# The first 128 tokens take no part in the matmuls with U: rows of U are made on chip, fetched, and multiplied on VectorE

## The chip, the cores and the metric

One core of a Trainium2 chip runs the whole program in one launch. The metric is the time of that launch on the device in microseconds; smaller is better. The program is the same on every run, and the time before is the median of three runs.

## The reference

Two layers of a decoder trunk with 512 tokens of width 1024, in float32. Each layer has a mixer (three parallel token mixers behind one wide projection, merged by gates), cross attention on 256 memory tokens, and PEER, a retrieval over 16384 experts of one neuron each:

```python
def peer(h, wq, keys, u_tab, v_tab):
    q = (h @ wq).reshape(bsz, length, 8, 2, 128)
    s = jnp.einsum('blhpd,hpkd->blhpk', q, keys)
    s_top, i_top = lax.top_k(s, 16)
    cand = s_top[..., 0, :, None] + s_top[..., 1, None, :]      # 16 x 16
    best, pos = lax.top_k(cand.reshape(..., 256), 16)           # per head
    gates = jax.nn.softmax(best, axis=-1)
    act = jax.nn.gelu(jnp.einsum('bthkd,btd->bthk', u_tab[idx], h)) * gates
    return jnp.einsum('bthk,bthkd->btd', act, v_tab[idx])
```

Every token so uses 8 x 16 = 128 experts, and for each a row of `u_tab` and a row of `v_tab`, both 1024 wide.

## The kernel before

All matmuls of any size are split into three products of a high and a low part (`fp32r`), so a weight tile passes ScalarE (the high part, a cast) and VectorE (the low part, a subtraction) before TensorE takes it. Each stage is a `Block` in which every engine runs its own list of instructions in order, tied to the others by semaphores. SyncE issues all plain DMAs in order, GpSimd the indirect ones.

**The projections** (`Linear`, lines 208 to 355; used by `normed_stage`, `linear_stage`, `gates_stage`, `residual_stage`, `keys_stage`). A weight tile of 2 MB has four units. For each unit ScalarE makes `w_hi` (L301), VectorE `w_lo` (L306), TensorE does 24 matmuls of 512 columns (L280 or L289). High and low parts have two buffers, so `w_lo` of a unit is made during the matmuls of the unit before, when those before that are done. SyncE loads a weight tile each four units and otherwise waits. In the mixer the first three stages are such projections, of 28, 8 and 24 units; `gates_stage` also stores each finished 1 MB tile of gates.

**Other stages**: HGRN, retention, S5 (`ssm_stage`, in which VectorE copies four row groups, then turns eight groups of injections, and SyncE copies 64 KB pieces with 32 DMAs, L1103), merge (24 short units of 12 matmuls), the output projection with the residual, then the query, attention (`attend_stage`, four heads) and its output.

**The keys stage** makes the scores and the top 16 keys for each head and side.

**The experts stage** (`experts_stage`) holds two loops of 128 tiles; a tile is 128 experts.

*The U loop.* Per tile n: SyncE loads U (512 KB, feature-major, three buffers), ScalarE makes `uh` (L1914), VectorE `ul` (L1986), TensorE does 24 matmuls of 512 columns, all tokens (L1856), ScalarE takes the GELU (L1920), SyncE stores the 128 x 512 result to `gelu_of_dots` in HBM. Beside this VectorE chooses the experts: `choose_keys` (tiles 2 to 5), then for each of four blocks of 128 tokens, eight tiles a block from tile 7: `pick_heads` (top 16 of 256 candidates for two heads, by MAX8, FIND_INDEX8 and MATCH_REPLACE8), `mark`, `soften`, `add_up` (a reduction, L2022). GpSimd makes the candidate sums (L1822) and the numbering product (L1831). From tile 45 to 92 VectorE makes the hot rows (`make_hot`, `weigh`: two 128x2048 f16 operations a tile, L2074, L2077, L2082), TensorE multiplies them to a dense table of gates (24 times 32 matmuls, L1877), and SyncE stores it in 12 pieces of 2 MB, one in four tiles, the last at tile 97. At tile 122 (`V0`) SyncE waits for gates and dots to be stored and loads the first three V tiles.

*The V loop.* Tokens 128 to 511 go through TensorE: activations times gates, split into parts, 18 matmuls of 512 columns a tile (L1888), with all rows of V. Tokens 0 to 127 stand apart (`APART = P`): each has a list of 128 experts; GpSimd fetches for list place c one dot per token from `gelu_of_dots` (L1843) and one row of V per token (L1844) into one of three buffers, and VectorE adds dot x gate x row to `acc` (`join`: L2052, L2058). In layer 0 VectorE also makes the tables of layer 1's S5 here.

SyncE's list in the U loop:

```python
for n in range(PK):
    if 1 <= n and n + 2 < PK:
        load_u(n + 2)
    if n:
        store_dots(n - 1)
    c, r = divmod(n - HOT0 - 8, 4)
    if 0 <= c < NH and r == 0:
        store_gates(c)
    if n == V0:
        ...
```

Of the kernel before, what the change touches and what calls it, by code (L numbers as in the profile page):

```python
# [35 lines left out]
SLOTS = PH * TOPK  # L36
GCH = 64
# [3 lines left out]
RING = 3  # L41
LEVELS = [64, 32, 16, 8, 4, 2, 1]
# [164 lines left out]

class Linear:
# [34 lines left out]
    def sync(self, sp, following=None, behind=None):  # L243

        def load(t, p, first):
            if not first:
                sp.wait_ge(self.s["lo_done"], (t - 1) * 4)
                self.weights.load(sp, t, p)
            if behind is not None and t >= 2:
                behind(sp, t - 2)  # L250
        over_pairs(sp, self.n, load)
        if following is not None:
            for t in (self.n, self.n + 1):
                sp.wait_ge(self.s["lo_done"], (t - 1) * 4)
                following.load(sp, t % 2, t % 2)
        if behind is not None:
            for t in range(max(self.n - 2, 0), self.n):
                behind(sp, t)
# [85 lines left out]
    def vector(self, v, copy=None, beside=None):  # L344
# [32 lines left out]
def setup_stage(nc, io, m, mem):  # L377

    with ExitStack() as ctx, stage(nc, "loaded", "dve_step", "angles_ready", "trig_ready") as s:
# [10 lines left out]
        with nc.Block() as block:  # L390
            @block.sync
            def _(sp):
                for dst, src in loads:
                    sp.dma_start(dst, src).then_inc(s["loaded"], 16)

# [123 lines left out]
def normed_stage(nc, m, gain, weights, act, psum, copy, following=None, ahead=None):  # L519


    with ExitStack() as ctx, stage(nc, *LINEAR_SEMS, *Norm.SEMS, "first_unit", weights=weights) as s:
        norm = Norm(nc, ctx, m, s, m.X, TB, [gain], [act], psum)
        lin = Linear(nc, ctx, s, "fm", weights, act, TB, T, psum, norm)
        with nc.Block() as block:
            @block.sync
            def _(sp):
# [3 lines left out]
                lin.sync(sp, following)  # L531
# [14 lines left out]
            def _(v):  # L546
# [3 lines left out]
                lin.vector(v)  # L550


def linear_stage(nc, kind, weights, act, nb, N, psum, copy, on="scalar", following=None):
    with ExitStack() as ctx, stage(nc, *LINEAR_SEMS, weights=weights) as s:
        lin = Linear(nc, ctx, s, kind, weights, act, nb, N, psum)
        with nc.Block() as block:
            block.sync(lambda sp: lin.sync(sp, following))
            block.tensor(lin.tensor)
            block.scalar(lambda a: lin.scalar(a, copy if on == "scalar" else None))
            block.vector(lambda v: lin.vector(v, copy if on == "vector" else None))  # L560
# [507 lines left out]
def ssm_stage(nc, m, sm, tabs, u, work, spare, rows, w_glu, psum):  # L1068
# [5 lines left out]
    with ExitStack() as ctx, stage(nc, "dve_step", "rows_mm", "sorted_even", "sorted_odd", "turn_mm", "turn_copied", "w_mm", "w_copied",  # L1074
                                   "inj_mm", "inj_turned", "scanned", "block_mm", "block_copied", "toep_in0", "toep_in1",
                                   "swap_mm", "states_in", "y_mm", "y_taken", "y_done", "yt_mm", "yt_copied",
                                   "out_mm", "out_copied", "glu_in") as s:
# [9 lines left out]
        wmat = [sb(f"wmat{i}", [P, 2, 2, P]) for i in range(2)]  # L1087
        om_, yb, st_ = (x.rearrange("p a t -> p (a t)").rearrange("p (g n) -> p g n", n=N5) for x in work)
# [8 lines left out]
        with nc.Block() as block:  # L1097
            @block.sync
            def _(sp):
                for c in range(NB):  # L1100
# [6 lines left out]
                sp.wait_ge(s["glu_in"], 16)  # L1107

# [118 lines left out]
            def _(v):  # L1227
                st = Steps(v, s["dve_step"])
                for b in range(NB):
                    v.wait_ge(s["rows_mm"], 2 * b + 2)  # L1230
                    sort_rows(v.tensor_copy, 2 * b + 1).then_inc(s["sorted_odd"], 1)
                for c in range(G5 // 4):
# [4 lines left out]
                    v.tensor_tensor(f2(om_)[:, cs], f2(om_)[:, cs], f2(st_)[:, cs], ALU.add).then_inc(s["inj_turned"], 1)  # L1237
                v.wait_ge(s["inj_turned"], G5 // 4)
# [1290 lines left out]
```

## Time and profile before

| | us |
|---|---|
| median of 3 runs | 4937.71 (4930.27 to 4955.9) |
| the profiled execution's own time | 4943.19 |
| its span in the profile | 4941.3 |
| TensorE busy | 4498.7 (91%) |
| TensorE weight loads | 3655.4 (74%) |
| VectorE busy | 2812.0 (57%) |
| ScalarE busy | 1698.1 (34%) |
| GpSimd busy | 816.6 (17%) |
| moved by DMA | 842.86 MB, 171 GB/s |

The page also cuts the span in 40 equal slices and gives each as a digit: tenths busy, tenths of TensorE's full clock, and GB/s. The two V loops are the slices of 263 to 350 GB/s; elsewhere the core moves 29 to 209 GB/s.

```profile
## 2 busy tenths in 40 slices
PE   5699888879999999988989997897999999999998
PEclk9899988999999999999999998898999999999999
DMA  4322114202445664887973221312224466479997
GB/s 179 145 101 111 47 71 128 102 29 83 143 144 177 209 197 160 320 295 283 350 297 119 85 107 71 94 69 85 90 91 145 154 204 207 164 263 346 338 350 270
```

A busy share of TensorE is that of instructions whose ends are modelled, so what a matmul costs in a stream is read from the distance between starts, not from its length.

### The profile page before, as it was taken

Reading aid. Unit: us, or ns where it says so; the run is one execution under the profiler, and the core shown is the slowest. Engines: PE = TensorE matmul, PEld = TensorE weight load, DVE = VectorE, ACT = ScalarE, POOL = GpSimd, SP = SyncE. Lnnn points to the kernel's source line nnn. Section 1 sums busy time; section 2 is a strip of 40 time slices with the busy share of each in tenths; the row PEclk is TensorE's granted clock in tenths of the full one; section 3 lists DMA queues with packets and bytes.
Section 4 is the critical chain, followed back from the end, with each engine's and each line's share of the span. In section 5 each row is a group of like instructions: output and inputs, shape, how many; then the busy total and the mean of one; then the engine's idle time right before and its main releaser. Section 6 shows DMA issues by size and latency. Waiting matters only on the chain. (4 is left out here: it accounts for less than half of the span.)

```text
span 4941.3 us, 54367 instructions
## 1 busy us (share of the span) xinstructions
PE 4498.7 (91%) x21288; PEld 3655.4 (74%) x21288; DVE 2812.0 (57%) x4695; ACT 1698.1 (34%) x2131; POOL 816.6 (17%) x588
## 2 busy tenths in 40 slices
PE   5699888879999999988989997897999999999998
PEld 4577766657888888766767775675778888887776
DVE  6522544427885532799872226353589554258887
ACT  3323222223335542332323232323233455233333
POOL 0000210000210000454530003000011000025554
PEclk9899988999999999999999998898999999999999
DMA  4322114202445664887973221312224466479997
GB/s 179 145 101 111 47 71 128 102 29 83 143 144 177 209 197 160 320 295 283 350 297 119 85 107 71 94 69 85 90 91 145 154 204 207 164 263 346 338 350 270
DMA packets 349246, 842.86 MB, mean 171 GB/s; under 512 B 31296, under 2 KB 191808, under 8 KB 333632
## 3 DMA queue, kind: packets, MB, share of 16 engines
q1 hardware_dynamic: 303936, 705.00, 40.7%
q0 software_dynamic: 45056, 134.38, 7.3%
q8 instruction: 170, 2.79, 0.2%
q14 instruction: 84, 0.69, 0.0%
HBM read 683.56 MB, written 151.52 MB: 169 GB/s over the span
## 5 line engine op out<-in xcount | busy, mean ns | idle before, releaser
L1986 DVE TENSOR_TENSOR ul<-u,uh 128x1024 fp32r<-128x1024 f32 x256 | 365.4, 1428 | 630.5 <-ACT uh L1914 628.3
L306 DVE TENSOR_TENSOR w_lo<-w,w_hi 128x1024 fp32r<-128x1024 f32 x200 | 244.3, 1225 | 729.3 <-ACT w_hi L301 728.0
L1888 PE MATMUL psum<-vh,ah 128*128 128x512 f32 x1536 | 486.3, 398 | 83.2 <-DVE al L2094 83.0
L1856 PE MATMUL psum<-h_lo,uh 128*128 128x512 f32 x2048 | 516.2, 394 | 13.3 <-DVE ul L1986 13.3
L1843 POOL DMA_INDIRECT pick_d<-gelu_of_dots,pick x256 | 276.2, 1079 | 1492.2 <-DMA gelu_of_dots<-ge 1076.2
L1856 PE MATMUL psum<-h_hi,ul 128*128 128x512 f32 x2048 | 506.3, 389 | 0.0
L1856 PE MATMUL psum<-h_hi,uh 128*128 128x512 f32 x2048 | 505.7, 389 | 0.0
L1888 PE MATMUL psum<-vl,ah 128*128 128x512 f32 x1536 | 479.8, 394 | 0.0
L1888 PE MATMUL psum<-vh,al 128*128 128x512 f32 x1536 | 478.2, 393 | 0.0
L1856 PEld LDWEIGHTS psum<-h_lo,uh 128*128 128x128 f32 x2048 | 381.6, 189 | 92.9 <-DVE ul L1986 15.8
L1945 ACT CAST vh<-v 128x1024 fp32r<-128x1024 f32 x256 | 269.3, 1052 | 524.2 <-PE psum L1888 444.7
L1856 PEld LDWEIGHTS psum<-h_hi,ul 128*128 128x128 f32 x2048 | 384.5, 188 | 81.0
L1856 PEld LDWEIGHTS psum<-h_hi,uh 128*128 128x128 f32 x2048 | 384.4, 188 | 79.8
L1888 PEld LDWEIGHTS psum<-vh,ah 128*128 128x128 f32 x1536 | 286.2, 191 | 167.7 <-DVE vl L2092 107.0
L1920 ACT ACTIVATE ge<-psum 128x512 f32<-128x512 f32 x256 | 153.7, 600 | 699.5 <-PE psum L1856 698.8
L2092 DVE TENSOR_TENSOR vl<-v,vh 128x1024 fp32r<-128x1024 f32 x256 | 312.9, 1222 | 123.8 <-ACT vh L1945 123.4
L1844 POOL DMA_INDIRECT rows<-in_peer_v,pick x256 | 333.6, 1303 | 88.0 <-issue 88.0
L1888 PEld LDWEIGHTS psum<-vl,ah 128*128 128x128 f32 x1536 | 292.3, 190 | 62.8
L1888 PEld LDWEIGHTS psum<-vh,al 128*128 128x128 f32 x1536 | 291.9, 190 | 62.5
L2058 DVE SCALAR_TENSOR_TENSOR acc<-rows,pick_d,acc 128x1024 f32<-128x1024 f32 x254 | 326.3, 1285 | 9.5 <-DVE pick_d L2052 0.5
L1914 ACT CAST uh<-u 128x1024 fp32r<-128x1024 f32 x256 | 266.6, 1043 | 171.1 <-DMA u<-in_peer_u 169.5
L301 ACT CAST w_hi<-w 128x1024 fp32r<-128x1024 f32 x200 | 209.2, 1050 | 183.6 <-PE psum L289 169.9
(421 smaller groups left out, 6817.7 us busy)
## 6 DMA issues: line engine op xcount, KB each, us to landing
u<-in_peer_u SPq DMA_DIRECT2D x256, 512.0 KB, 3.7
v<-in_peer_v SPq DMA_DIRECT2D x256, 512.0 KB, 6.2
gelu_of_dots<-ge SPq DMA_DIRECT2D x256, 256.0 KB, 2.2
gates_by_group<-held SPq DMA_DIRECT2D x24, 2048.0 KB, 9.8
act<-gelu_of_dots SPq DMA_DIRECT2D x64, 768.0 KB, 7.5
gate<-gates_by_group SPq DMA_DIRECT2D x64, 768.0 KB, 9.7
w<-in_w_fm SPq DMA_DIRECT2D x12, 2048.0 KB, 8.1
w<-in_w_gate SPq DMA_DIRECT2D x12, 2048.0 KB, 8.1
```

Of the source, the lines that this page charges most:

```text
L301: a.copy(self.shaped(self.hi[q % 2]), self.unit_of(p, q)).then_inc(self.s["hi_done"], 1)
L306: v.tensor_tensor(self.shaped(self.lo[q % 2]), self.unit_of(p, q), self.shaped(self.hi[q % 2]).bitcast(F32), ALU.subtract).then_inc(self.s ...
L1843: pool.indirect_dma_start(pick_d[:, c:c + 1], None, every_dot, bass.IndirectOffsetOnAxis(ap=pick[:, 1, c:c + 1], axis=0)).then_inc(m.rows_ ...
L1844: pool.indirect_dma_start(rows[c % NG][:], None, every_v, bass.IndirectOffsetOnAxis(ap=pick[:, 0, c:c + 1], axis=0)).then_inc(m.rows_picke ...
L1856: mm = nc.tensor.matmul(dot_bank(n), w[r][:, k, :], h[:, k, :], start=(x == 0 and k == 0), stop=(x == 2 and k == KD - 1))
L1888: mm = nc.tensor.matmul(sum_bank(b, half), q[p][:, b * P:(b + 1) * P], w[p][:, half * W:(half + 1) * W], start=(n == 0 and x == 0), stop=( ...
L1914: a.copy(fw(uh[r]), u[r][:]).then_inc(s["u_hi"], 1)
L1920: a.activation(ge[n % 2][:], dot_bank(n), ACT.Gelu_apprx_tanh).then_inc(s["gelu_done"], 1)
L1945: a.copy(vh[p][:], vv[n % VR][:]).then_inc(s["v_hi"], 1)
L1986: v.tensor_tensor(fw(ul[r]), u[r][:], fw(uh[r]).bitcast(F32), ALU.subtract).then_inc(s["u_lo"], 1)
L2058: v.scalar_tensor_tensor(acc[:], rows[c % NG][:], pick_d[:, c:c + 1], acc[:], ALU.mult, ALU.add).then_inc(s["joined"], 1)
L2092: v.tensor_tensor(vl[p][:], vv[n % VR][:], vh[p][:].bitcast(F32), ALU.subtract).then_inc(s["v_lo"], 1)
```

## The change

Tokens 0 to 127 leave the U loop's matmuls as they had left the V loop's.

1. *Turned rows of U.* U lies in HBM feature-major, for the matmuls. The new class `Turns` loads a tile of 512 KB, turns its 32 x 32 blocks with one VectorE transpose, and stores it with four DMAs (32 partitions each, runs of 256 numbers) as rows in `m.u_rows[l]`. It has two raw and one or two (in some stages three or four) outgoing buffers. The features of a row so lie in another order, and `h0`, the normed tokens in that order, is made to match in the keys stage. 124 of the 128 tiles of each layer are turned beside the projections, S5, merge and attention of that layer, 4 in its keys stage. Each stage ends with a wait for its stores.
2. *The dots of tokens 0 to 127.* For list place c GpSimd fetches one row of U per token in the U loop (one of four buffers), VectorE multiplies it with `h0` and sums it up (`dot`), 128 times over the tiles 21 to 127; ScalarE takes the GELU in four chunks. The dense result and `gelu_of_dots` now have 384 columns. The fetch of single dots goes. The rows of V follow in the same ring right behind.
3. *The choosing.* 80 of the 256 candidates remain (those that can be in the top 16), GpSimd does none of it, the reduction becomes four additions, and the steps are laid out anew: keys at tiles 1, 3, 5, 8, the first block from 10, the others from 20 to 74 in steps of 9/4 tiles, hot rows from 75 in steps of 11/12 tile, the last table store at 122, `V0` at 123.
4. `gates_stage` holds its gates in halves; the list of SyncE in `Linear.sync` goes by units; the gains of the expert norm go to HBM as a row in the setup.

The core of the diff:

```diff
+class Turns:
+    def load(self, sp, x):
+        if x < self.n:
+            if x >= 2:
+                sp.wait_ge(self.s["row_turned"], x - 1)
+            sp.dma_start(self.raw[x % 2], self.src(x)).then_inc(self.s[f"turn_in{x % 2}"], 16)
...
+    def behind(self, sp, u):
+        for x in [x for x in range(self.n) if self.after[x] == u]:
+            p = x % len(self.out)
+            sp.wait_ge(self.s["row_turned"], x + 1)
+            for b in range(P // S):
+                sp.dma_start(self.dst(x)[b], self.out[p][b * S:(b + 1) * S].rearrange("p (f w) -> p f w", f=P // S)).then_inc(self.s[f"turn_out{p}"], 16)
+            self.load(sp, x + 2)
+
+    def turn(self, v, u):
+        for x in [x for x in range(self.n) if self.after[x] == u]:
+            p = x % len(self.out)
+            v.wait_ge(self.s[f"turn_in{x % 2}"], 16 * (x // 2 + 1))
+            if x >= len(self.out):
+                v.wait_ge(self.s[f"turn_out{p}"], 16 * (P // S) * (x // len(self.out)))
+            v.transpose(self.out[p],
+                        self.raw[x % 2].rearrange("p (k f w) -> p f k w", k=KD, w=S)).then_inc(self.s["row_turned"], 1)
+
+    def done(self, sp):
+        for p in range(len(self.out)):
+            sp.wait_ge(self.s[f"turn_out{p}"], 16 * (P // S) * len(range(p, self.n, len(self.out))))
...
+        for u in range(4 * self.n):
+            t = u // 4 + 2
+            if u % 4 == 3 and (t < self.n or following is not None):
+                sp.wait_ge(self.s["lo_done"], u + 1)
...
+            if turns is not None:
+                turns.behind(sp, u)
...
+                if turns is not None:
+                    turns.turn(v, t * 4 + q)
...
+                turns.start(sp)
+                for x in range(3 * NB):
+                    turns.behind(sp, x)
                 for c in range(NB):
                     sp.wait_ge(s["block_copied"], 2 * c + 2)
...
+                    if n == 2:
+                        v.wait_ge(s["gain_in"], 16)
+                        as_rows = lambda x: x.rearrange("p (k b w) -> p b k w", k=KD, b=P // S)
+                        v.tensor_tensor(h0[:].rearrange("p (b k w) -> p b k w", b=P // S, k=KD), as_rows(norm.xn[:, 0, :]), as_rows(gain_row[:]), ALU.mult)
...
+KEYS_AT = [1, 3, 5, 8]
+HOT0, V0, JOIN0 = 75, 123, 4
...
-                    pool.indirect_dma_start(pick_d[:, c:c + 1], None, every_dot, bass.IndirectOffsetOnAxis(ap=pick[:, 1, c:c + 1], axis=0)).then_inc(m.rows_picked[c % NG], 16)
-                    pool.indirect_dma_start(rows[c % NG][:], None, every_v, bass.IndirectOffsetOnAxis(ap=pick[:, 0, c:c + 1], axis=0)).then_inc(m.rows_picked[c % NG], 16)
+                for x in range(2 * SLOTS):
+                    if x >= NG:
+                        before = x - NG
+                        if before < SLOTS:
+                            pool.wait_ge(s["dotted"], before + 1)
+                        else:
+                            pool.wait_ge(s["joined"], before - SLOTS + 1)
+                    c = x % SLOTS
+                    pool.indirect_dma_start(rows[x % NG], None, m.u_rows[l] if x < SLOTS else every_v,
+                                            bass.IndirectOffsetOnAxis(ap=pick[:, x // SLOTS, c:c + 1], axis=0)).then_inc(m.rows_picked[x % NG], 16)
...
-                            mm = nc.tensor.matmul(dot_bank(n), w[r][:, k, :], h[:, k, :], start=(x == 0 and k == 0), stop=(x == 2 and k == KD - 1))
+                            mm = nc.tensor.matmul(dot_bank(n), w[r][:, k, :], h[:, k, T0:], start=(x == 0 and k == 0), stop=(x == 2 and k == KD - 1))
...
+                def dot(c):
+                    v.wait_ge(m.rows_picked[c % NG], fetched(c))
+                    v.scalar_tensor_tensor(rows[c % NG], rows[c % NG], 1.0, h0[:], ALU.mult, ALU.mult,
+                                           accum_out=pick_d[:, c:c + 1]).then_inc(s["dotted"], 1)
...
-                normed_stage(nc, m, sm[:, 0:KD], w_fm, h, psum, fm_out, following=w_tm)
+                normed_stage(nc, m, sm[:, 0:KD], w_fm, h, psum, fm_out, turning(sorted([*range(2, 28), *range(5, 28, 4)])),
+                             tm[:].rearrange("p (a b) n -> p a (b n)", b=2), following=w_tm)
```

## Rows read from the trace of the kernel before

**Rows 1.** The page, part 1: busy time of each engine.

```profile
PE 4498.7 (91%) x21288; PEld 3655.4 (74%) x21288; DVE 2812.0 (57%) x4695; ACT 1698.1 (34%) x2131; POOL 816.6 (17%) x588
```

**Rows 2.** Busy time by stretch: stretch, length, engines with counts, clock, DMA share, GB/s.

```profile
215.00:345.00 130.00, 130.00 (x561) 105.42 (x560) 28.60 (x24) 41.05 (x54) 0.00 (x0) 1.00 0.26 97
1342.00:1500.00 158.00, 157.07 (x697) 129.54 (x696) 132.44 (x206) 52.92 (x71) 32.08 (x7) 1.00 0.43 145
1600.00:1700.00 100.00, 100.00 (x630) 83.65 (x629) 53.07 (x47) 54.32 (x38) 0.00 (x0) 1.00 0.67 209
1976.00:2350.00 374.00, 330.81 (x1373) 261.10 (x1373) 327.96 (x494) 118.17 (x158) 189.55 (x156) 0.97 0.82 299
2350.00:2530.00 180.00, 166.05 (x712) 133.97 (x711) 143.42 (x205) 63.21 (x82) 97.53 (x85) 0.98 0.96 360
4500.00:4920.00 420.00, 403.42 (x1754) 328.66 (x1753) 348.90 (x498) 145.09 (x194) 237.50 (x199) 1.00 0.91 334
```

**Rows 3.** Matmuls of U and V by line: durations, first and last start.

```profile
L1856 PE MATMUL psum<-h_lo,uh x2048: 387/389/794, 1229.4 to 4370.0; 128*128 128x512 f32 x187
L1888 PE MATMUL psum<-vh,ah x768: 387/389/767, 1977.0 to 2588.9; 128*128 128x512 f32 x192
L1888 PE MATMUL psum<-vh,ah x768: 389/389/628, 4373.8 to 4923.0; 128*128 128x512 f32 x192
```

**Rows 4.** TensorE in order of time, 256 and 512 columns, products; a weight load.

```profile
61.83 1.12 PE L2307 MATMUL psum<-memT_hi,w_lo 128*128 128x256 f32 x8
62.79 1.12 PE L2307 MATMUL psum<-memT_hi,w_hi 128*128 128x256 f32 x8
...
L2307 PEld LDWEIGHTS psum<-memT_hi,w_lo x128: 188/192/330, 49.2 to 140.1; 128*128 128x128 f32 x128
...
1403.47 1.98 PE L1856 MATMUL psum<-h_hi,ul 128*128 128x512 f32 x8
1405.29 1.98 PE L1856 MATMUL psum<-h_hi,uh 128*128 128x512 f32 x8
...
1756.98 2.02 PE L1877 MATMUL psum<-part,hot_j 128*128 128x128 f16 x32
```

**Rows 5.** Groups of VectorE by shape: busy us, mean ns, idle before.

```profile
L2058 DVE SCALAR_TENSOR_TENSOR acc<-rows,pick_d,acc 128x1024 f32<-128x1024 f32 x254 | 326.3, 1285 | 9.5 <-DVE pick_d L2052 0.5
L2082 DVE TENSOR_TENSOR part<-hot_i,lists 128x2048 f16<-128x2048 f16 x96 | 113.0, 1219 | 0.0
L2022 DVE TENSOR_REDUCE out<-hot 128x128 f32<-128x2048 f16 x16 | 65.1, 4069 | 0.0
L2052 DVE TENSOR_TENSOR pick_d<-pick_d,pick_w 128x1 f32<-128x1 f32 x256 | 40.0, 156 | 66.6 <-DMA rows<-in_peer_v,pick 64.8
L1564 DVE MAX8 val<-sc 128x8 f32<-128x128 f32 x128 | 27.8, 279 | 0.2
L1564 DVE MAX8 best<-cand 128x8 f32<-128x256 f32 x64 | 23.9, 415 | 0.0
```

**Rows 6.** DMA issues with us to landing, and GpSimd's wait before its gathers.

```profile
u<-in_peer_u SPq DMA_DIRECT2D x256, 512.0 KB, 3.7
gates_by_group<-held SPq DMA_DIRECT2D x24, 2048.0 KB, 9.8
...
POOL pick_d L1843 <- DMA gelu_of_dots<-ge: 1076.2, 2, 538.6
```

**Rows 7.** VectorE in order of time in the first projection.

```profile
283.24 1.23 DVE L306 TENSOR_TENSOR w_lo<-w,w_hi 128x1024 fp32r<-128x1024 f32 x1 [4.35 <-ACT w_hi L301]
288.82 1.23 DVE L306 TENSOR_TENSOR w_lo<-w,w_hi 128x1024 fp32r<-128x1024 f32 x1 [4.36 <-ACT w_hi L301]
```

**Rows 8.** S5: a stretch of its copies, SyncE's issues, VectorE at an injection.

```profile
750.00:755.00 5.00, 5.00 (x24) 2.23 (x23) 4.93 (x4) 2.00 (x2) 0.00 (x0) 1.00 0.75 94
...
743.44 21.76 SPq L1103 DMA_DIRECT2D toep<-fm  x32
...
721.27 0.42 DVE L1235 TENSOR_TENSOR fm<-psum,tcos 128x256 f32<-128x256 f32 x1 [1.81 <-PE psum L1145]
```

More of the change, by code:

```diff
@@ L241, in first_loads, with sync @@
         self.weights.load(sp, 1, 1)
[L243 to L258, printed above, removed]
+    def sync(self, sp, following=None, behind=None, turns=None):
+        for u in range(4 * self.n):
+            t = u // 4 + 2
+            if u % 4 == 3 and (t < self.n or following is not None):
+                sp.wait_ge(self.s["lo_done"], u + 1)
+                if t < self.n:
+                    self.weights.load(sp, t, t % 2)
+                else:
+                    following.load(sp, t % 2, t % 2)
+            if behind is not None:
+                behind(sp, u)
+            if turns is not None:
+                turns.behind(sp, u)
     def tensor(self, pe):
@@ L1099, in _ @@
             def _(sp):
+                turns.start(sp)
+                for x in range(3 * NB):
+                    turns.behind(sp, x)
                 for c in range(NB):
@@ L1231, in _ @@
                     sort_rows(v.tensor_copy, 2 * b + 1).then_inc(s["sorted_odd"], 1)
+                    turns.turn(v, b)
                 for c in range(G5 // 4):
@@ L1320, in _ @@
             def _(sp):
-                lin.sync(sp, None, rest_tile)
-                for p in range(2):
-                    sp.wait_ge(rested[p], 16 * (weights.n // 2))
+                turns.start(sp)
+                lin.sync(sp, None, rest_behind, turns)
+                rest_half(sp, weights.n - 1, 1)
+                for half in range(2):
+                    sp.wait_ge(rested[half], 16 * weights.n)
+                turns.done(sp)
             block.tensor(lin.tensor)
@@ L1383, in _ @@
             def _(sp):
-                for t in range(2, weights.n + 2):
-                    sp.wait_ge(s["w_lo"], HALF * (t - 1))
-                    if t < weights.n:
-                        weights.load(sp, t, t % 2)
-                    else:
-                        following.load(sp, t - weights.n, t % 2)
+                turns.start(sp)
+                for n in range(NU):
+                    if n % HALF == HALF - 1:
+                        t = n // HALF + 2
+                        sp.wait_ge(s["w_lo"], n + 1)
+                        if t < weights.n:
+                            weights.load(sp, t, t % 2)
+                        else:
+                            following.load(sp, t - weights.n, t % 2)
+                    turns.behind(sp, n)
+                turns.done(sp)
             @block.tensor
@@ L1461, in _ @@
                         sum_low(n - 19)
+                    turns.turn(v, n)
                 weigh(NU - 1)
@@ L1475, in attend_stage, with _ @@
         pt = [sb(f"probT{i}", [P, MB, T]) for i in range(2)]
+        turns = turning(s, ctx, None)
         mx, sm_, rc = sb("mx", [P, XH, TB]), sb("sme", [P, XH, TB]), sb("rc", [P, XH, TB])
         with nc.Block() as block:
+            @block.sync
+            def _(sp):
+                turns.start(sp)
+                for x in range(3 * XH):
+                    turns.behind(sp, x)
+                turns.done(sp)
             @block.tensor
@@ L1717, in experts_stage @@
                 ab = tmp("ab", [P, 2, SLOTS], F16)
-                hot = [two(f"hot{i}", hkk, F16) for i in range(2)]
+                rc = tmp("rc", [P, 2, SLOTS], F16)
+                far, wrap, near = (tmp(n, [P, SLOTS], F16) for n in ("far", "wrap", "near"))
+                hot = two("hot", hkk, F16)
                 numbers = tmp("numbers", [P, TOPK])
```

405 lines of the change are left out of this document (241 added, 164 removed).

## The prediction

> **What bounds the kernel now.** I read the page first, then the busy time by stage, then the time order inside one unit of each loop, then the DMA rows. TensorE is busy 91% of the span [rows 1], and by stage it is the limit almost everywhere that this change touches: 130 of 130 us in the first projection, 157 of 158 and 100 of 100 us in two stretches of the loop over U [rows 2]. The expert layer is two loops of 128 tiles. The U loop of layer 0 runs from 1229.4 to 1977.0 us (the first V matmul), 747.6 us, and that of layer 1 is alike. The V loops take 613 us in layer 0 and 551 in layer 1 [rows 3]. A U tile is 24 matmuls of 512 columns; eight of them follow each other in 1.81 us [rows 4], so a tile is 5.44 us and 128 tiles 696. The 24 products of the gate table (32 matmuls in 2.0 us each [rows 4]) bring it to 744. So the U loop is TensorE's, with no room. A V tile is 18 matmuls, 4.08 us, or 522 us a loop: layer 1 loses 29 us to waits, layer 0 loses 91, where VectorE also makes the tables of the next layer (328 of 374 us busy [rows 2]). All sums are against the profiled execution: span 4941.3, its own time 4943.2, which is 5.5 us over the median of the three.
>
> **U loop, TensorE.** 128 of the 512 columns go. The price of a column comes from the memory stage: eight matmuls of 256 columns take 0.96 us, 0.120 each, eight of 512 take 0.2265 each [rows 4]. That is 0.000416 us a column, so 384 columns take 0.173 us and a tile 4.16 us: 1.28 us less, 163.5 us a layer, **327 us** in both. A weight load of this size is shown as 0.192 us, longer than 0.173; but it is shown so beside the 256-column matmuls too, and they run 0.120 us apart [rows 4]. So the load is hidden and I take 0.173. The Trainium skill (TensorE: Matmul & The Clock Gate, Back-to-back issue gap) says that a stream of load and matmul pairs is spaced by both operations, which speaks against this change; the 0.120 us of this trace is against it for these sizes.
>
> **U loop, VectorE.** It loses GpSimd's company but gains its work. Per tile: `low_u` 1.2 us. Per token row, 128 of them over 106 tiles: one multiply with a row sum, 128x1024 with two inputs, priced as the accumulate at 1.285; that is 1.55 us a tile. The top-16 searches go from 256 to 80 candidates: an instruction takes 0.415 at 256 and 0.279 at 128 [rows 5], 0.051 off for another 48 gives 0.23. With overlap a pair of heads goes from 3.8 to about 2.0 us. The numbering comes over from GpSimd at 1.22 (two a block), and the 4.07 us reductions become four adds, about 1.5. A block of tokens costs about 20 us instead of some 31. Between tiles 21 and 74: 54 x (1.2 + 1.55) + 3 x 20 = 208 us against TensorE's 225. Between 75 and 119, where the hot rows are made (48 steps of 2.4): 115 + 45 x 2.75 = 239 us against TensorE's 45 x 4.16 + 48 = 235. So VectorE goes from half busy to level with TensorE, and I charge 8 us a layer for uneven tiles.
>
> **U loop, DMA.** Now 0.43 busy before the hot rows, 2.3 us for 0.79 MB a tile; 0.67 in them [rows 2], 4.3 us a tile of 6.4, so a 2 MB store of gates, one in four tiles, takes 8 us. The V rows and tiles run at 334 GB/s with 0.91 busy, 367 GB/s full, 1.43 us for 0.52 MB. After: U tile 1.43, dots 0.65 (384 of 512 columns of what is left of 2.3), 1.2 gathered rows 1.72, together 3.8 us in a tile of 4.16; in the hot tiles one store each 3.7 tiles adds 2.2, together **6.0 us against VectorE's 5.3**. DMA becomes the bound there: 45 x 0.7, +30 us a layer. At the tail the last gate store now leaves at tile 122 and SyncE waits for it at 123 (before: 97 and 122), with three V tiles and two groups ahead of the last two U tiles. Gates take 9.8 us to land [rows 6], 3 MB follow in 8 us: U tile 126 is about 22 us after 123 and wanted after 10, so +11. The first tiles: +1. **Given back: 50 us a layer**, bounds 15 (the engines share better than the sum) and 100. Net for the U loops: -227, bounds -297 and -127.
>
> **V loop.** The 256 gathers of one number and the small multiplies go (0.156 us and a gap, 24 us of VectorE a loop [rows 5]), the rows' first fetches are already under way. TensorE's 522 stays. Layer 0 is VectorE's: -20. Layer 1: -10 of its 29. **-30**, bounds -55 and -5.
>
> **The turns.** 124 of 128 tiles of a layer are turned outside the keys stage: 32 in the first projection, 8 and 28 in the next two, 12 each in S5, merge and attention, 20 in the two residuals and the query. Each adds a 0.5 MB load, a VectorE transpose, four stores and, on SyncE, five issues. No transpose is in the trace: the nearest rows are 1.285 for 1024 elements and two inputs and 4.07 for 2048 strided ones [rows 5], so 1.28 to 2.03 us; I take 1.3, since this one reads nearly in order too. The Trainium skill (VectorE: DVE Perf Modes, The three transpose paths) gives 0.31 us for a 128x128 block of 16-bit numbers; no run here shows it. In a projection unit of 5.58 us VectorE idles 4.35 us before each `w_lo` [rows 7], so one turn or two hide if their data is there. If it isn't, `w_lo` queues behind the wait on VectorE, and TensorE behind that. Whether it is there is DMA's question. Load 1.43; the stores have runs of 1 KB from 32 partitions. Dots, 2 KB runs from 128 partitions, would give 1.8 us for 0.5 MB; the copies from 16 partitions in S5 run at 94 GB/s with 0.75 busy [rows 8], 4.2 us. I take 2.2, nearer the dots since their destination is HBM too, so 3.6 us a turn. The three projections last about 325 us and need 68 x 3.6 + 15 weight tiles x 5.6 + 20 for gates = 349 us. That is **+24**, and +6 for uneven ones; bounds 5 and 165. S5: its first four turns meet a phase of 1.7 us a step and each pair waits for five issues (0.68 each by the S5 copies [rows 8]) and a landing (3.7 [rows 6]): +12; at the next eight VectorE idles 1.81 us each [rows 8], enough for the transpose. Merge +6, its VectorE being fuller; attention +3, other stages, with their stores awaited at the end, +4. **+55 a layer, +110**, plus 3 for the gains at the start. Bounds +30 and +410.
>
> **Sum:** -227 - 30 + 110 + 3 = -144 on 4941.3; median 4937.7 - 144 = **4795**, rounded to 5.
>
> **Rivals.**
> (a) *All of it hides.* Requests overlap better than my sums: U loops -290, V -45, turns +45: 4650. For it: DMA stands 0.96 busy at 360 GB/s in one stretch of the V loop while TensorE is 166 of 180 busy [rows 2]. Against it: 3.6 us x 68 has no room.
> (b) *The U loop passes to VectorE and DMA,* so that fewer columns buy little: VectorE level with TensorE and DMA 0.9 or more together cost another 45 us a layer: 4880. For it: the V loop of layer 0, where VectorE at 328 of 374 us leaves TensorE 331 [rows 2]. Against it: layer 1 loses only 5% with DMA 0.91 busy.
> (c) *Slower: the stores of the turned rows.* If their price is that of the S5 copies, a turn is 5.6 us, the projections need 68 x 5.6 + 104 = 485 us for 325: +160 a layer, S5, merge and attention +45: 4941 - 257 + 410 = 5090. It decides from the point where the turns give back 257 us, 128 a layer: 25 of these are fixed, so 103 / 68 = 1.5 us over the 3.25 us that are free (325 - 104 over 68), a turn of 4.8 us and a store of 3.3.
> (d) *The weight load sets the pace.* 24 x 0.192 = 4.61 us a tile, 57 us a layer less saved, of which 30 lie under the DMA's excess: 4850. Only the spacing of 0.120 us speaks against it, and it is clear.
>
> **Numbers.** Forecast 0.47 (4720 to 4850), (a) 0.18, (b) 0.20, (c) 0.10, (d) 0.05. About 0.5% (25 us) is what a measurement of this kernel can tell from no change. Of (b) a quarter lies within that: faster 0.85, same 0.05, slower 0.10. The range of 8 in 10 runs from 4640, under (a), to 4920, over (b).
>
> **What would show it.** Matmuls of line 1856's successor 0.17 us apart and U tiles 4.2 us apart before the hot rows, about 6.0 within them, with DMA at 0.9 or more; a gap of some 10 us in TensorE near tile 126; U loops of about 635 us. GpSimd's wait of 538 us before the gathers [rows 6] gone. The first three stages 25 to 30 us longer, with VectorE waiting for the raw tile of a turn at the double turns; transposes at 1.2 to 2.0 us. It is wrong if these stages grow by over 100 us a layer (then (c)), if the U tiles stay above 4.5 us before the hot rows with VectorE full (then (b)), or if the projections keep their length (then (a)).

## The result and the profile after

The change made the kernel 0.8% slower: 4975.4 us (4956.3 to 4982.7) against 4934.1 (4914.7 to 4955.9), a ratio of 1.008 with the interval 1.007 to 1.0094, where 4795 was forecast and 4640 to 4920 allowed for. The profiled execution spans 4977.0 us.

The page, part 1 and two lines of part 2, of the kernel after:

```profile
PE 4250.9 (85%) x21282; PEld 3630.8 (73%) x21282; DVE 3255.4 (65%) x5347; ACT 1662.7 (33%) x2135; POOL 758.1 (15%) x564
...
PEclk9899988989999988999999998799899998899999
DMA  4597726666288877988988882566536887789997
```

TensorE was relieved of 248 us [rows 1] and the span is 36 us longer all the same: the engine has less work and stands still for longer. Where, I read from the distance between the first matmuls of each stage, in both traces and in four kernels of the experiments, which are told below (us, the sum of the two layers; S5 runs to the start of merge, a V loop to the next projection or the end; HGRN, retention, the attention's own output and the keys are not in the table and moved by 6 us at most):

| stage | before | after | early | early_pool | moved_sync | noturn |
|---|---|---|---|---|---|---|
| three projections | 708.5 | 764.1 | 759.4 | 762.7 | 761.3 | 709.9 |
| S5 | 219.7 | 259.1 | 260.3 | 261.1 | 238.5 | 210.4 |
| merge | 156.5 | 187.0 | 185.4 | 185.0 | 187.3 | 157.3 |
| output and query | 217.6 | 220.9 | 222.4 | 221.6 | 236.8 | 218.0 |
| attention | 108.1 | 135.1 | 132.7 | 132.6 | 114.5 | 107.0 |
| U loops | 1495.8 | 1414.9 | 1278.2 | 1199.4 | 1198.1 | 1422.1 |
| V loops | 1195.0 | 1149.8 | 1145.2 | 1149.2 | 1144.4 | 1151.9 |
| span | 4941.3 | 4977.0 | 4827.1 | 4756.6 | 4731.6 | 4822.1 |

From before to after: U loops -81 (forecast -227), V loops -45 (-30), everything else +162 (forecast: turns +110 and setup +3). Two stretches of the U loop of layer 0 after the change, ahead of the hot rows and in them (columns as in [rows 2]):

```profile
1410.00:1640.00 230.00, 225.12 (x1294) 223.09 (x1293) 200.54 (x449) 90.39 (x124) 94.75 (x64) 1.00 0.90 314
1640.00:1980.00 340.00, 259.14 (x1871) 252.23 (x1870) 226.41 (x253) 151.91 (x118) 83.48 (x56) 0.88 0.78 254
```

Ahead of the hot rows all is as forecast. In them TensorE stands for 81 of 340 us, its clock is 0.88, and no engine is full: VectorE 226, DMA 0.78. Something makes all of them wait. The waits of that stretch (us in total, how many, the longest), then ScalarE, SyncE and TensorE in order of time around one of them:

```profile
POOL rows L1963 <- DVE rows L2199: 252.4, 47, 16.5
ACT uh L2032 <- DMA u<-in_peer_u: 174.0, 26, 15.7
DVE ul L2110 <- ACT uh L2032: 111.3, 20, 10.5
PE psum L1997 <- ACT held L2060: 76.5, 13, 11.8
```

```profile
1789.18 0.49 ACT L2038 ACTIVATE ge<-psum 128x384 f32<-128x384 f32 x1 [2.25 <-PE psum L1976]
1800.83 1.04 ACT L2032 CAST uh<-u 128x1024 fp32r<-128x1024 f32 x1 [11.15 <-DMA u<-in_peer_u]
1801.78 3.72 ACT L2060 ACTIVATE held<-psum 128x2048 f32<-128x2048 f32 x1
```

```profile
1777.73 0.66 SPq L1905 DMA_DIRECT2D gelu_of_dots<-ge  x1
1778.43 0.43 SPq L1901 DMA_DIRECT2D u<-in_peer_u  x1
1786.03 0.32 SPq L1905 DMA_DIRECT2D gelu_of_dots<-ge  x1
1786.39 0.62 SPq L1909 DMA_DIRECT2D gates_by_group<-held  x1
1787.05 6.26 SPq L1901 DMA_DIRECT2D u<-in_peer_u  x1
1793.35 1.12 SPq L1905 DMA_DIRECT2D gelu_of_dots<-ge  x1
1794.52 0.94 SPq L1901 DMA_DIRECT2D u<-in_peer_u  x1
1805.84 0.32 SPq L1905 DMA_DIRECT2D gelu_of_dots<-ge  x1
```

```profile
1797.83 1.55 PE L1976 MATMUL psum<-h_hi,uh 128*128 128x384 f32 x8
1805.64 3.57 PE L1997 MATMUL psum<-part,hot_j 128*128 128x128 f16 x32 [6.26 <-ACT held L2060]
```

These rows show a loop of waits. SyncE's list for tile n is: load U tile n+2, store the dots of n-1, perhaps a store of gates. The load of tile n+2 so stands behind the store of dots n-2, which waits for its GELU, and ScalarE wants the tile one tile of work later, ahead of GELU n. If it isn't there, GELU n, the copy of the gate table and the store of dots n queue behind that wait, and with them the load of tile n+4. A landing (5.5 us in the median after, 6.7 in this stretch, 3.7 before [rows 6]) must fit in about one tile, which is now 4.2 us of TensorE's work, or 5.2 with its share of the products. And the issue that follows a store of gates is held up: 6.26 us here, 5.5 to 9.6 us at all 24 stores; and SyncE, done with its next load at 1795.5, waits 10 us for a GELU, which stands behind ScalarE's wait of 11.15 us for a U tile. TensorE then runs its 32 products at half the pace (3.57 us for 2.0).

The kernel before has the same held-up issues (5.4 to 7.0 us, all 24), and nothing shows that they cost it anything: TensorE works 100 of 100 us among them [rows 2]. The same place there, SyncE in order of time:

```profile
1706.83 0.43 SPq L1772 DMA_DIRECT2D gates_by_group<-held  x1
1707.31 5.79 SPq L1764 DMA_DIRECT2D u<-in_peer_u  x1
1713.86 0.51 SPq L1768 DMA_DIRECT2D gelu_of_dots<-ge  x1
```

How much each part of a U loop takes over TensorE's own work (4.16 us a tile, 2.0 a product) can be read from the starts of its tiles; layer 0, layer 1, in us:

| tiles of the U loop | forecast | after | early | pool | early_pool |
|---|---|---|---|---|---|
| 0 to 74, ahead of the hot rows | 1 | 10, 13 | 3, 3 | 7, 10 | 4, 3 |
| 75 to 121, the hot rows | 30 | 101, 96 | 37, 39 | 64, 59 | 0, 0 |
| 122 to 127, the tail | 11 | 16, 18 | 18, 18 | 25, 24 | 16, 16 |

(The forecast has 8 more for VectorE, at no place.) In the hot rows of the kernel after a tile takes 7.3 us on the mean, against 6.0 forecast.

### The profile page after: what moved, and what is told of

The parts are those of the page before. It is cut to its first block and busy times, and to the rows that moved or that the text cites. A ratio compares the mean times of both kernels' runs of the same rounds, so it can differ in the third digit from the quotient of the medians.

```text
span 4977.0 us, 56515 instructions
## 1 busy us (share of the span) xinstructions
PE 4250.9 (85%) x21282; PEld 3630.8 (73%) x21282; DVE 3255.4 (65%) x5347; ACT 1662.7 (33%) x2135; POOL 758.1 (15%) x564
## 5 line engine op out<-in xcount | busy, mean ns | idle before, releaser
L1963 POOL DMA_INDIRECT rows<-rows_of_u,pick x256 | 374.0, 1461 | 2223.8 <-DVEq L2195 1387.4
L2110 DVE TENSOR_TENSOR ul<-u,uh 128x1024 fp32r<-128x1024 f32 x256 | 313.0, 1224 | 377.3 <-ACT uh L2032 376.2
L1976 PE MATMUL psum<-h_lo,uh 128*128 128x384 f32 x2048 | 425.5, 351 | 51.9 <-DVE ul L2110 51.8
L1963 POOL DMA_INDIRECT rows<-in_peer_v,pick x256 | 287.6, 1124 | 792.3 <-DVE acc L2216 709.5
L1976 PE MATMUL psum<-h_hi,ul 128*128 128x384 f32 x2048 | 402.2, 338 | 0.0
L1976 PE MATMUL psum<-h_hi,uh 128*128 128x384 f32 x2048 | 396.7, 334 | 0.0
L1976 PEld LDWEIGHTS psum<-h_hi,ul 128*128 128x128 f32 x2048 | 365.8, 191 | 0.0
L1976 PEld LDWEIGHTS psum<-h_hi,uh 128*128 128x128 f32 x2048 | 359.1, 188 | 0.0
L253 DVE STREAM_TRANSPOSE turn<-turn 128x1024 f32<-128x1024 f32 x146 | 181.1, 1241 | 223.0 <-DMA turn<-in_peer_u 156.6
L2199 DVE SCALAR_TENSOR_TENSOR rows<-rows,h 128x1024 f32<-128x1024 f32 x256 | 308.8, 1218 | 2.0
## 6 DMA issues: line engine op xcount, KB each, us to landing
gates_by_group<-held SPq DMA_DIRECT2D x24, 2048.0 KB, 12.7
```

The source lines that it names most:

```text
L253: v.transpose(self.out[p], self.raw[x % 2].rearrange("p (k f w) -> p f k w", k=KD, w=S)).then_inc(self.s["row_turned"], 1)
L1963: pool.indirect_dma_start(rows[x % NG], None, m.u_rows[l] if x < SLOTS else every_v, bass.IndirectOffsetOnAxis(ap=pick[:, x // SLOTS, c:c ...
L1976: mm = nc.tensor.matmul(dot_bank(n), w[r][:, k, :], h[:, k, T0:], start=(x == 0 and k == 0), stop=(x == 2 and k == KD - 1))
L2110: v.tensor_tensor(fw(ul[r]), u[r][:], fw(uh[r]).bitcast(F32), ALU.subtract).then_inc(s["u_lo"], 1)
L2199: v.scalar_tensor_tensor(rows[c % NG], rows[c % NG], 1.0, h0[:], ALU.mult, ALU.mult, accum_out=pick_d[:, c:c + 1]).then_inc(s["dotted"], 1)
```

## Experiments

The kernel before was measured anew beside each group of experiments and its median went from 4934.1 to 4924.6 us, while the kernel after was measured beside the first of these values alone; so a difference from it is good to some 10 us.

**Theory A**: the order of SyncE's queue. **Rival B**: DMA throughput, as the prediction had it for the hot tiles. **Rival C**: VectorE, now level with TensorE. The first four kernels tell them apart and price the turns.

*early*: only the order of the loads changes.

```diff
-                    if 1 <= n and n + 2 < PK:
-                        load_u(n + 2)
+                    if n + 3 < PK:
+                        load_u(n + 3)
```

> SyncE issues the load of each U tile one tile sooner (tile n+3 instead of n+2, before the store of the dots of tile n-1); nothing else changes. Theory A (order of SyncE's queue): in the kernel after, the load of U tile n+2 stands behind the store of the dots of tile n-2, which waits for ScalarE's gelu, and ScalarE needs the tile one tile later, so landing (5.5 us) plus a blocked issue behind a store of gates (6 to 9 us) stalls the loop. Then the hot stretch 1640:1980, 340 us at 259 us of TensorE, shrinks by 50 to 80 us a layer: 4975 - 100 to 160, about 4840. Rival B (DMA throughput is the bound of the hot tiles): the same bytes, so the same time within 15 us: 4975. Rival C (VectorE is the bound of the hot tiles): the same, 4975.

4836.1 us, 0.981 of before (0.978 to 0.984) and 139 less than after, as theory A had it. The U loops give 137 of it. No byte and no VectorE work is gone, so B and C can't account for this part. The stretch of the hot rows:

```profile
1640.00:1940.00 300.00, 257.21 (x1888) 250.79 (x1888) 222.60 (x253) 158.03 (x121) 82.42 (x58) 0.94 0.92 306
```

*pool*: only the issuer of the 24 stores of gates changes.

```diff
-                    for c in stores_at[n]:
-                        store_gates(c)
...
+                def store_gates(c):
+                    pool.wait_ge(s["gate_copied"], 2 * c + 2)
+                    pool.dma_start(gates_dram[:, :, c, :].rearrange("g p x -> p g x"),
...
+                    while stored < NH and (x >= SLOTS + NG or x >= NG and min(stores_at_c[stored], PK) <= dot_at(x - NG)):
+                        store_gates(stored)
+                        stored += 1
```

> The 12 stores of gates a layer (2 MB each) are issued by GpSimd between its gathers instead of by SyncE; the U loads stay where they were. Theory A in its narrow form (the issue behind a store of gates blocks SyncE for 6 to 9 us): 24 stores x 6 us less, if each was felt in full: about -100 to -140, 4850. If only the missing lead of the loads counts and the block is secondary: -30 to -60. Rival B (DMA throughput) and rival C (VectorE): 4975 within 15 us.

4908.1 us, 0.995 (0.994 to 0.997), 67 less than after: half to two thirds of what the narrow form asked for, a little over the other. No issue of a U load takes over 2 us any more, and GpSimd's issue of a store of gates takes 1.75. The edit also takes SyncE's wait for the copied gates out of its list, but that wait was worth nothing: in the kernel after SyncE issues each of the 24 stores 0.04 us behind the issue ahead of it. The Trainium skill (DMA: Bandwidth & Descriptors, Issuing engines are not separate DMA queues) says that DMAs of all engines interleave on the same 16 DMA engines, and that another issuer saves only the sequencer's time, "which is usually small relative to the DMA itself". No run here tests the first half. Against the second, the time saved on SyncE was 5.5 to 9.6 us a store, beside 12.7 us from the issue of a store of gates to its landing, and worth 67 us.

*nofetch*: of the 128 fetches of rows of U in a layer only the first four are made, and VectorE multiplies these four again and again; the fetches of V then wait for the last multiply. The dots of tokens 0 to 127 are left wrong.

```diff
-                for x in range(2 * SLOTS):
+                for x in [*range(NG), *range(SLOTS, 2 * SLOTS)]:
...
-                    v.wait_ge(m.rows_picked[c % NG], fetched(c))
+                    v.wait_ge(m.rows_picked[c % NG], fetched(c % NG))
...
```

> Of the 128 gathers of U rows a layer only the first four are done; VectorE multiplies these four again and again (the dots of the first 128 tokens are left wrong), so its work and its order stay. 62 MB a layer less traffic during the U loop, a third of it. Rival B (DMA throughput is the bound of the hot tiles): -30 us to -60 a layer, about 4880. Theory A: a landing gets shorter, but the order stays: -10 to -30 a layer. Rival C (VectorE): no change, 4975.

4885.8 us, 90 less than after, 46 to 50 a U loop: inside B's range, not A's. So the traffic does matter. U tiles land after 3.9 us in the median here, against 5.5, so it can work by way of the landing, within A's loop of waits; this run alone doesn't tell the two apart. But a third of the traffic gone gives less than one reordered line.

*noturn*: no turns. In this run, and in *nostore* and *quarter*, the rows are fetched from U as it is given, and the dots of tokens 0 to 127 are left wrong.

```diff
-        self.s, self.after, self.first = s, after, m.rows_made[l]
+        self.s, self.after, self.first = s, [], m.rows_made[l]
...
-        self.n = len(after)
+        self.n = 0
...
```

> All 248 turns outside the keys stage and those inside it are left out (no load, transpose or store of them); the U rows are fetched from the U given in DRAM, which has them in another order, so the dots of the first 128 tokens are left wrong. It prices the turns by stage: I read about 158 us for both layers from the two traces (three projections 55, S5 40, merge 30, attention 25, others 8). If they are the turns' own: 4975 - 158 = 4817, and every stage as long as before the change. If part of the growth is a lower clock or DMA traffic that comes from elsewhere: 4860 or more. The U loop (708 us) should not change.

4821.2 us, 154 less. In the sum of both layers every stage of the table but S5 and the loops is within 1.5 us of its length before; S5 is 9 shorter, all of it in layer 0, where this profile shows a granted clock of 0.96 in the stage and before one of 0.86. The U loops gain nothing by it. The turns cost about what the stages showed.

The next four ask what is left in early, whether before had this loss too, and of what a turn's price is made.

*early_pool*: both edits.

> Both: U loads one tile sooner on SyncE, and the stores of gates issued by GpSimd. The run early brought a U loop from 708 to 638 us, the run pool to 676, each against about 595 us of TensorE work (128 tiles of 4.16 and 24 products of 2). Theory A (what is left in early, stalls of 5 to 8 us at some stores of gates, is the blocked issue behind these stores): 600 to 615 us a U loop, 4836 - 50 to 70 = about 4775. Rival B (what is left is DMA throughput, 0.94 busy in the hot stretch): no more than 10 us a loop below early, 4820 to 4836.

4760.5 us, 0.967 (0.964 to 0.969), 76 less than early. The U loops take 600.6 and 598.8 us, and the hot rows nothing over TensorE's own work: 5.2 us a tile. ScalarE's wait in the hot stretch, the stretch itself, and GpSimd in order of time:

```profile
ACT uh L2040 <- DMA u<-in_peer_u: 39.1, 23, 3.0
```

```profile
1640.00:1900.00 260.00, 250.63 (x1946) 246.15 (x1944) 226.18 (x257) 163.83 (x120) 112.55 (x71) 0.99 0.99 356
```

```profile
1702.98 1.68 POOL L1971 DMA_INDIRECT rows<-rows_of_u,pick  x1 [2.88 <-DVE rows L2207]
1704.65 1.75 POOL L1955 DMA_DIRECT2D gates_by_group<-held  x1
1707.53 1.71 POOL L1971 DMA_INDIRECT rows<-rows_of_u,pick  x1 [1.13 <-DVE rows L2207]
```

The longest wait for a U tile is 3.0 us where it was 15.7, the clock is back at 0.99, and DMA, 0.78 busy in after, does 0.99 at 356 GB/s while TensorE works 251 of 260 us. The throughput that B held to be the bound was there all the time and wasn't asked for. It is close to being one now. A U tile lands after 10 us in the median of this stretch, later than in after (6.7), and the longer lead holds it.

*before_early*: the edit of early in the kernel before.

> The kernel before, with its U loads issued one tile sooner and nothing else. Its U tiles are 5.4 to 6.4 us long, so that a landing and a blocked issue fit behind them; its U loop of 747 us is filled by TensorE. Theory A: no gain, 4929 within 10 us: the order of the queue cost nothing before the change and is a cost that the shorter tiles uncovered. Rival: the order cost the kernel before as well, a gain of 20 us or more; then early owes part of its 140 us to something that was there all along.

4931.4 us, ratio 1.0006 (0.999 to 1.002). The order cost nothing until the tiles grew short.

*early_smalldot*: early, with VectorE's multiply at an eighth of its width (its dots are left wrong).

```diff
-v.scalar_tensor_tensor(rows[c % NG], rows[c % NG], 1.0, h0[:], ALU.mult, ALU.mult,
+v.scalar_tensor_tensor(rows[c % NG][:, 0:P], rows[c % NG][:, 0:P], 1.0, h0[:, 0:P], ALU.mult, ALU.mult,
```

> The kernel early with the multiply of each fetched U row cut from 1024 to 128 columns (the dots of the first 128 tokens are left wrong): 128 x about 1.0 us less for VectorE in each U loop, all transfers as before. If VectorE holds back what is left (638 us a loop against some 595 of TensorE work): 10 to 25 us a loop less, 4800. If it doesn't (theory A, and DMA as rival B): within 5 us a loop, 4836.

4839.6 us, 3.5 over early and within its spread. Of 300 us in the hot stretch VectorE works 165 instead of 223 and no engine gets further for it: C is out.

```profile
1640.00:1940.00 300.00, 257.08 (x1891) 250.48 (x1890) 165.39 (x245) 156.00 (x119) 68.06 (x56) 0.93 0.93 306
```

*nostore*: loads and transposes, no stores.

```diff
-            for b in range(P // S):
-                sp.dma_start(self.dst(x)[b], ...).then_inc(self.s[f"turn_out{p}"], 16)
```

> As the kernel after, with loads and transposes of all turns but without their stores (the U rows come from the U given in DRAM, in another order, so that the dots of the first 128 tokens are left wrong). The turns cost 154 us together (run noturn). If it is the stores (in S5 VectorE waits 3 us at 11 turns for the last store, since there is one buffer for turned rows; in the projections 0.5 MB each): projections 355 + 5, S5 back from 130 to about 112, merge still 88 or more, all in all 4975 - 80. If it is VectorE's 1.24 us in front of the next w_lo: every stage stays within 3 us, 4975 - 20. I expect S5 and the projections to be the stores' and merge and attention VectorE's.

4853.4 us, 122 less than after, where I had expected 80; of the turns' 154 only 32 are left. Per layer: projections 354 and 353 (from 387 and 377), S5 117 (130), attention 54 (68), merge 90 (93). So the stores account for nearly all in projections and attention, though in attention I had expected it of VectorE. In S5 I had expected 112. In merge 11 to 12 of 15 us stay without the stores. The transposes take 12 x 1.24 us of VectorE there, and before the change VectorE worked 52 of the stage's 78 us, 2.2 us in a unit of 3.3; that these 11 us are the transposes' is likely by that, but not shown, since the loads stay too. After the change, VectorE in S5 (one buffer for turned rows: it waits for the last store to land), and the group of the transposes:

```profile
762.19 1.25 DVE L253 STREAM_TRANSPOSE turn<-turn 128x1024 f32<-128x1024 f32 x1 [3.58 <-DMA rows_of_u<-turn]
766.39 0.42 DVE L1308 TENSOR_TENSOR fm<-psum,tcos 128x256 f32<-128x256 f32 x1 [2.95 <-PE psum L1217]
```

```profile
L253 DVE STREAM_TRANSPOSE turn<-turn 128x1024 f32<-128x1024 f32 x146 | 181.1, 1241 | 223.0 <-DMA turn<-in_peer_u 156.6 <-DMA rows_of_u<-turn 66.0
```

The last four: are the stores dear by their bytes or by SyncE's order, as in the U loop, and by their place?

*turns_pool*: early_pool, with the stores of turned rows issued by GpSimd.

```diff
+    def stores(self, pool):
+        for x in range(self.n):
+            p = x % len(self.out)
+            pool.wait_ge(self.s["row_turned"], x + 1)
+            for b in range(P // S):
+                pool.dma_start(self.dst(x)[b], ...).then_inc(self.turned_out[p], 16)
```

> As early_pool (4760 us), and GpSimd also issues the stores of all turned rows; SyncE keeps the loads. Run nostore showed that the stores cost 28 us a layer in the projections, 13 in S5, 13 in attention and 4 in merge. If that is the order of SyncE's queue again (the load of the next tile to be turned, and the weights, stand behind a wait for VectorE and four issues): projections and attention lose most of it, 20 to 35 us a layer, 4760 - 40 to 70 = about 4705. If it is the traffic itself (DMA 0.83 to 0.88 busy in the projections): no change there, 4760 within 12 us. S5 has one buffer for turned rows, and VectorE waits for each landing: no change there in either case.

4811.6 us, 51 more than early_pool; neither case had foreseen that. The projections are 8 us longer in the sum (770.4; 780 in *moved*, against 758 to 764 in the kernels with all of the stores on SyncE), S5 28 (288.7): a store that GpSimd issues lands after 3.9 us instead of 2.7, and S5 waits for each. The cure of the U loop is none here.

*quarter*: 32 of 128 KB in each store.

```diff
-                sp.dma_start(self.dst(x)[b], self.out[p][b * S:(b + 1) * S].rearrange("p (f w) -> p f w", f=P // S)).then_inc(...)
+                sp.dma_start(self.dst(x)[b][:, 0:1, :], self.out[p][b * S:(b + 1) * S].rearrange("p (f w) -> p f w", f=P // S)[:, 0:1, :]).then_inc(...)
```

> As the kernel after, but each of the 992 stores of turned rows writes only the first quarter of its rows (32 KB instead of 128); the number of issues and the waits stay (the U rows come from the U given in DRAM, in another order, so the dots of the first 128 tokens are left wrong). It tells bytes from issues in the projections, where the stores cost 28 us a layer (run nostore). If it is the traffic: the projections fall from about 382 to 362 or less, near the 354 without stores. If it is the issues and their order on SyncE: they stay within 5 us of 382. S5 waits for each landing, fixed cost included: 130 to about 123.

4899.1 us, 76 less than after. The projections fall to 358.0 and 358.1: with all of the issues and waits and a quarter of the bytes, nearly all of the cost is gone. A quarter of the bytes is also a quarter of the pieces of 1 KB, so the run doesn't tell bytes from pieces. S5 is at 122.5, half way to its length without stores, and attention at 61 and 63, a third to a half of the way: there the number of stores, kept in this run, costs too. DMA in the three projections of layer 0, after, then quarter, then nostore:

```profile
211.00:598.00 387.00, 348.68 (x1441) 277.40 (x1442) 165.78 (x161) 105.79 (x136) 0.13 (x1) 0.96 0.84 272
```

```profile
211.00:569.00 358.00, 340.31 (x1440) 273.05 (x1440) 165.90 (x162) 105.80 (x135) 0.00 (x0) 0.98 0.65 220
```

```profile
212.00:566.00 354.00, 339.82 (x1441) 273.07 (x1441) 164.08 (x161) 105.33 (x135) 0.00 (x0) 0.98 0.56 196
```

From 0.65 busy to 0.84 the projections lose 29 us (19 in layer 1): it is the traffic, which makes the raw tiles land later (4.8 us in after, 4.0 in quarter), and VectorE waits for them ahead of the next `w_lo`, 116 us in this stretch after the change and 55 in quarter.

*moved*: turns_pool with 12 turns a layer moved.

```diff
-                          tm[0:N5, :, :], tile_at(io["w_glu"], l), psum, turning(range(12)))
+                          tm[0:N5, :, :], tile_at(io["w_glu"], l), psum, turning([4, 5, 6, 7, 8, 9, 10, 11]))
-            attend_stage(nc, m, l, qT, kT, v_tm, o_parts, psum, turning(range(12)))
-            residual_stage(nc, m, w_o, o_parts, psum, turning(range(1, 8)))
+            attend_stage(nc, m, l, qT, kT, v_tm, o_parts, psum, turning([1, 4, 7, 10]))
+            residual_stage(nc, m, w_o, o_parts, psum, turning([1, 1, 2, 3, 3, 4, 5, 5, 6, 7]))
...
```

> As turns_pool, and turns change their place: S5 keeps 8 of 12 (none in its first phase), attention 4 of 12; the two residual stages take 10 instead of 7 each, the query 9 instead of 6, the keys 7 instead of 4. If the price of a turn is set by its place (in the traces 1.7 us each in S5, 1.0 in attention, 0.1 in residuals and query): 12 turns leave places that cost about 15 us a layer for places that cost 1 to 3, so 20 to 28 us less than turns_pool. If the new places are as dear once they are doubled (DMA 0.66 busy in them): the same as turns_pool within 8 us.

4775.4 us, 36 less than turns_pool by the medians, more than foreseen, and 27 by the profiled executions: S5 32 and attention 21 shorter, output and query 14 and the projections 9 longer.

*moved_sync*: the same places, stores on SyncE.

> The places of run moved, with the stores of turned rows back on SyncE (the U loads one tile sooner and the stores of gates on GpSimd, as in early_pool). Run turns_pool showed that stores issued by GpSimd land later (3.9 against 2.7 us) and that S5 pays 14 us a layer for it; run moved showed 27 us less than turns_pool by the places alone. If the two effects add: 4760 - 25 = 4735, S5 about 120, attention about 58, out and query 117. If the new places cost more with SyncE's stores, whose queue also brings the weights there: 4760.

4732.9 us, 0.960 of before (0.958 to 0.963), 28 less than early_pool, where 25 was foreseen if the two effects add: they do. S5 is at 119, attention at 57; output and query, with 19 turns for 13, pay 7.6 us a layer more, the attention's own output and the keys, with 17 for 11, 3.5: a cheap place stays cheap only up to its slack. This is the fastest kernel of the study: with the order mended, the stores of gates on GpSimd and the turns in better places, the change is worth 4%, some 190 us, where as it was made it costs 41.

## Why the prediction was wrong

**The step that failed** is "Given back: 50 us a layer" in the U loop; it was 122 to 124 (163.5 saved, 40 to 41 seen). Within it the term "DMA becomes the bound there: 45 x 0.7, +30 us" failed: the hot rows lost 96 to 101. Its mechanism was wrong, not its size alone. I charged the hot tiles with 6.0 us for DMA's throughput, 0.7 a tile over VectorE's 5.3; the runs show a queue's order: 68 a loop for the late loads (early), 39 more for the held-up issue (early_pool), and 15 left. The split depends on what is mended first: the stores alone gave 33 a loop (pool). With both mended a hot tile takes 5.2 us, all of its transfers included, so the 6.0 was too high as a price too. The U loops then take 600, below the forecast of about 635, and the 15 that are left lie in the tail: TensorE waits 14 us ahead of the last U tile, whose load stands in SyncE's list behind the wait for the last gates and three V tiles. That is the forecast's +11, right in mechanism and nearly in size (16 to 18). The rows for the right reading stood in the trace of the kernel before. I had priced the landing of a U tile (3.7 us) and of gates (9.8) [rows 6] and looked at SyncE for the tail, but never asked how much time the list leaves between the issue of a load and its use, nor how long the issue itself takes. Whoever makes a tile a quarter shorter must ask this of each wait in it.

Term by term, in us over both layers:

- *Columns, -327*: right. Matmuls start 0.173 us apart ahead of the hot rows, as forecast. A weight load is shown with 188 to 198 ns and is hidden, so rival (d) is out. The rule of the Trainium skill (TensorE: Matmul & The Clock Gate, Back-to-back issue gap), that both operations set the spacing, doesn't decide here.
- *VectorE's part of the U loop*: right in size (`dot` 1.22 us for 1.285; 201 of 230 us busy against 208 of 225), and no bound (early_smalldot), so that its 8 us stood for nothing.
- *V loops, -30*: -45, inside the bounds.
- *Turns, +110*: +158 by the stages, 154 by noturn. The transpose is 1.24 us (forecast 1.3). The three projections, +30 a layer, came to 32 and 23, but that is luck in part. The sum set 349 us of DMA against stages of about 325; in the trace of the kernel before they last 354, so the sum's own +24 would have been nothing. And DMA is not full in them after the change (0.84 busy). What holds is that the turns' traffic sets the cost (quarter), by tiles that land late for VectorE. Too small were S5 (12, came to 20: each turn waits for a landing, not each pair), merge (6, came to 15, of which 4 come with the stores) and attention (3, came to 14 with 12 turns in bursts of three; its stores account for it). I had given these stages a lump each; the stages show that a turn costs from 0.1 us (output, query) to 1.6 (S5).
- *Sum*: U loops 146 off, turns and setup 49, V loops 15 the other way: 180, the whole of the error.

**The rivals.** (c), the slower side, had been tied to the price of a store: it asked for a turn of 4.8 us. Turns were nowhere near +410. The slower result came from the other half of the sum, which had no rival on that side: (b) let the U loop pass to VectorE or DMA at 45 us more a layer, and its size was even too small (the loops lost 73 more each), but neither engine was full. A fourth rival was missing: the loop through SyncE, GELU and the landing.

**What would show it**, as written: U tiles 4.2 us apart ahead of the hot rows came true; "about 6.0 within them, with DMA at 0.9 or more" failed on both halves (7.3 us and 0.78), and DMA at 0.78 with TensorE at 0.76 is what told that no throughput was the bound. U loops of 635 us failed (708 and 707). The gap near tile 126 came, and so did VectorE's wait for raw tiles in the projections.

Left open: why the issue behind a 2 MB store of gates is held up at all, and whether smaller stores on SyncE would avoid it (not tried). The granted clock in S5 differs between executions (0.86 and 0.96 above), which moves that stage by some 10 us a layer, and isn't explained.

## What to carry to other kernels

When a change shortens the tile of a loop, measure every lead in tiles, not in microseconds: for each load, the time from its issue to its use must hold its landing and whatever its queue does in between. If no engine is near full and DMA isn't either, as here with TensorE at 0.76, VectorE at 0.67 and DMA at 0.78, look for a circle of in-order queues before blaming throughput; moving one line in an issuing engine's list is the cheapest test of it. Background work goes where the engine that does it and DMA both have slack: the same turn cost 0.1 us in one stage and 1.6 in another.

## What the runs showed of the hardware

The DMA issue that follows a 2 MB store in pieces of 512 B on SyncE took 5.4 to 10.7 us in every one of 24 cases of each kernel that I looked at (before, after, early), against 0.43 in the median of the U loads. Issued by GpSimd, the same store's own issue took 1.75 us, and no issue of a U load on SyncE over 2 us. Small stores (128 KB, pieces of 1 KB) landed later by GpSimd, 3.9 against 2.7 us. DMA reached 356 GB/s at 0.99 busy over 260 us with loads, gathers and stores mixed.
